# Swapped halves by small DMAs for the rotary embedding, instead of a rotation product

## The chip, the cores and the metric

The kernel runs on one core of a Trainium2 chip. The metric is the time of one execution in device microseconds. The text is about five engines of the core: TensorE (matrix products, PE in the profile), VectorE (DVE), ScalarE (ACT), GpSimd (POOL) and SyncE (SP), which here only issues DMAs. Each engine works through its own program in order; engines meet only at semaphores. A DMA's data is moved by 16 DMA engines once SyncE has issued it.

## The reference

Two blocks run on 512 tokens of width 1024. The second has two layers, each with four kinds of attention whose queries and keys partly get a rotary embedding:

```python
def apply_rope(z, cos, sin):
    ...
    z1, z2 = jnp.split(z, 2, axis=-1)
    return jnp.concatenate([z1 * c - z2 * s, z1 * s + z2 * c], axis=-1)
```

It is applied to heads of 64 columns (`cos_h`), to 32 columns of each latent-attention head (`cos_r`) and to index heads of 32 columns (`cos_i`). So every element is multiplied by a cosine, and the element half a head away, with a sign, by a sine; the two are added.

## The kernel before

All activations lie transposed in SBUF: features on the 128 partitions, 512 tokens in the free dimension. A head's two halves are therefore on different partitions, 32 or 16 rows apart.

**Weights** come as slabs of 8 tiles of 128 x 128 (512 KB) in the order of use. `load_slabs` (L521) lets SyncE fetch them into three raw buffers: slab n may be fetched when the buffer of slab n - 3 is free. For most slabs, ScalarE writes a rounded high half (`high_slabs`, L545, 128 x 1024) and GpSimd or VectorE the low half (`low_slabs`, L560); then the raw buffer is free (`w_lo_made`), and TensorE makes three products for each tile, high by high, high by low and low by high. A few slabs ("plain") are used unsplit in the two-pass format of 32 bits, and their buffer is free only when their last product is done (`sums_done`). In ScalarE's program the high half of the slab two ahead stands before the eviction of the job at hand, so the eviction waits if that slab has not landed.

**The feature stage** (`gemm_phase`, L611 and after, called by `Layer.features` with `banks=3` and `between=Features`) runs once in each of the two layers. Its jobs, in order: kvcmp, dki, iq0, iq1, cq0, cq1, ckv, kk, nq0, nq1, dq0, dq1, sq0, sq1 (8 tiles, 24 products each), then mq0 to mq3 (2 plain tiles), four uk jobs (1 plain tile each) and two token jobs (uv). A job sums into one of three PSUM banks, and ScalarE evicts it to its tile in `big` (L693, signals `taken`). Thirteen jobs have a rope: kvcmp, dki, iq0, iq1, kk, nq0, nq1, dq0, dq1 and mq0 to mq3. For these

- TensorE, after the products of the next job, multiplies the evicted tile by a 128 x 128 rotation matrix into bank 4 or 5 (`rotate`, L651, signals `rotated`);
- VectorE multiplies that bank by the sine table into a scratch tile (L714), the tile by the cosine table in place (L716), and adds the two (L718, signals `joined`).

Between jobs, `Features` puts work of its own: hidden products of the compression (L2556, plain slabs, after iq1, cq0, cq1 and ckv), index scores (L2690, evicted by L2699, added up by VectorE at L2714), sums of squares of two norms (L836, from squares at L865), halves of keys on GpSimd (L2754). It waits for `joined` counts where it needs roped tiles.

The order of each engine's program is what the loops write; there is no scheduler. At the end of the stage a barrier (L392) holds all engines until each is through, and attention begins (L1882 on TensorE), whose own jobs use the next slabs. The rope tables and rotation matrices (`rope`, 4608 columns) are loaded into `big` ahead of the stage (L753).

## Time and profile before

| | us |
|---|---|
| median of three runs | 3346.08 (3340.59 to 3346.92) |
| profiled execution, span from first to last instruction | 3349.0 |
| TensorE busy in the span | 3244.9 |
| VectorE busy | 1487.5 |
| ScalarE busy | 1272.6 |
| GpSimd busy | 384.3 |
| DMA, slabs of weights | 503 issues of 512 KB |

The profiled execution is one of its own; its span is 2.9 us above the median, and what lies outside the span is not shown. The busy time of an engine counts overlapping matmuls once. The granted clock of TensorE over the span is 0.989 of full speed. The stage that the change touches lasts about 120 us in each of the two layers, and ends at 1605 us and at 2729 us of the span.

### The profile page before, as it was taken

The numbers are of one execution on the slowest core, as the hardware profiler recorded it, in microseconds if no ns is written. First come the engines' busy times: TensorE is split into PE (matmuls) and PEld (weight loads), VectorE is DVE, ScalarE is ACT, GpSimd is POOL, SyncE is SP. The second block draws the span as 40 slices with busy tenths as digits, with TensorE's granted clock in tenths as the row PEclk, the third lists the DMA queues.
The fourth block names the chain that finished last, engine by engine and source line by source line (L and its number), as shares of the span: only waits on it lengthen the run. The fifth ranks groups of instructions, "written<-read, shape, count | busy, mean of one in ns | idle before, by whom it ended". The sixth has DMA issues, their size and how long they took to land. (4 is left out here: it accounts for less than half of the span.)

```text
span 3349.0 us, 37289 instructions
## 1 busy us (share of the span) xinstructions
PE 3244.9 (97%) x14860; PEld 2566.0 (77%) x14860; DVE 1487.5 (44%) x2324; ACT 1272.6 (38%) x2190; POOL 384.3 (11%) x277
## 2 busy tenths in 40 slices
PE   9999999999999999999979999999999998899998
PEld 7767678878888888877656888878887766578886
DVE  4154523244243333355875533343334478563333
ACT  3344643233232223235655423242222456542222
POOL 0411324410000000002510000000000243000000
PEclk9998999999999999999989999999999999999999
DMA  4211213323333333332001232323332310023332
GB/s 154 88 44 38 88 58 106 96 87 95 101 95 99 96 99 92 99 104 88 26 1 63 88 96 93 100 87 96 95 95 88 129 45 1 27 88 95 97 94 74
DMA packets 76061, 276.92 MB, mean 83 GB/s; under 512 B 8688, under 2 KB 8944, under 8 KB 75632
## 3 DMA queue, kind: packets, MB, share of 16 engines
q1 hardware_dynamic: 75888, 274.54, 26.5%
q8 instruction: 118, 1.93, 0.2%
q14 instruction: 55, 0.45, 0.0%
HBM read 272.41 MB, written 2.10 MB: 82 GB/s over the span
## 5 line engine op out<-in xcount | busy, mean ns | idle before, releaser
L545 ACT ACTIVATE w_hi<-raw_slabs 128x1024 fp32r<-128x1024 f32 x489 | 516.7, 1057 | 1236.5 <-PE ps L585 1128.8
L560 DVE TENSOR_TENSOR w_lo<-raw_slabs,w_hi 128x1024 fp32r<-128x1024 f32 x372 | 454.8, 1223 | 717.3 <-ACT w_hi L545 717.2
L585 PE MATMUL ps<-in_hi,w_hi 128*128 128x512 f32 x1840 | 719.5, 391 | 5.0 <-DVE in_lo L911 5.0
L585 PE MATMUL ps<-in_hi,w_lo 128*128 128x512 f32 x1840 | 716.3, 389 | 0.0
L585 PE MATMUL ps<-in_lo,w_hi 128*128 128x512 f32 x1840 | 716.2, 389 | 0.0
L585 PE MATMUL ps<-parts,w_hi 128*128 128x512 f32 x2240 | 693.9, 391 | 0.9 <-DVE scratch L1528 0.8
L560 POOL TENSOR_TENSOR w_lo<-raw_slabs,w_hi 128x1024 fp32r<-128x1024 f32 x117 | 287.7, 2461 | 2315.2 <-ACT w_hi L545 2298.1
L585 PEld LDWEIGHTS ps<-parts,w_hi 128*128 128x128 f32 x2240 | 420.5, 188 | 92.6 <-issue 4.3
L585 PE MATMUL ps<-parts,w_lo 128*128 128x512 f32 x1120 | 436.0, 389 | 0.0
L585 PEld LDWEIGHTS ps<-in_hi,w_hi 128*128 128x128 f32 x1840 | 345.5, 188 | 83.2 <-DVE in_lo L911 9.2
L585 PEld LDWEIGHTS ps<-in_lo,w_hi 128*128 128x128 f32 x1840 | 345.5, 188 | 72.0 <-issue 1.0
L585 PEld LDWEIGHTS ps<-in_hi,w_lo 128*128 128x128 f32 x1840 | 345.5, 188 | 71.6
L585 PEld LDWEIGHTS ps<-parts,w_lo 128*128 128x128 f32 x1120 | 210.3, 188 | 43.6
L667 PE MATMUL ps<-in_hi,w_hi 128*128 128x512 f32 x584 | 236.8, 405 | 1.6 <-POOL w_lo L560 1.4
L667 PE MATMUL ps<-in_hi,w_lo 128*128 128x512 f32 x584 | 227.7, 390 | 0.0
L667 PE MATMUL ps<-in_lo,w_hi 128*128 128x512 f32 x584 | 227.7, 390 | 0.0
L1314 DVE SCALAR_TENSOR_TENSOR big<-ps,scratch 128x512 f32<-128x512 f32 x88 | 60.6, 691 | 267.8 <-PE ps L585 248.6
L667 PEld LDWEIGHTS ps<-in_hi,w_hi 128*128 128x128 f32 x584 | 109.7, 188 | 32.0 <-issue 6.8
L667 PEld LDWEIGHTS ps<-in_lo,w_hi 128*128 128x128 f32 x584 | 109.7, 188 | 25.4 <-issue 3.8
L667 PEld LDWEIGHTS ps<-in_hi,w_lo 128*128 128x128 f32 x584 | 109.7, 188 | 23.3
L2059 ACT ACTIVATE scratch<-ps,stats 128x384 f32<-128x384 f32 (+4 forms) x176 | 85.3, 485 | 99.7 <-DVE stats L2032 73.2
L1890 PE MATMUL ps<-const_cols,scratch 128*128 128x128 f32 (+1 forms) x472 | 94.1, 295 | 20.6 <-ACT scratch L1938 17.3
(303 smaller groups left out, 3579.4 us busy)
## 6 DMA issues: line engine op xcount, KB each, us to landing
raw_slabs<-weights SPq DMA_DIRECT2D x503, 512.0 KB, 3.6
big<-rope SPq DMA_DIRECT2D x2, 2304.0 KB, 8.8
x_resid<-xT SPq DMA_DIRECT2D x8, 256.0 KB, 5.0
outT<-x_resid SPq DMA_DIRECT2D x8, 256.0 KB, 2.0
const_cols<-consts SPq DMA_DIRECT2D x1, 836.0 KB, 9.6
scratch<-brow SPq DMA_DIRECT2D x1, 768.0 KB, 9.4
vector_cols<-vec SPq DMA_DIRECT2D x2, 45.5 KB, 9.9
vector_cols<-vec SPq DMA_DIRECT2D x1, 68.5 KB, 3.1
```

The costliest lines, as they stand in the source:

```text
L545: self.nc.scalar.activation(self.w_hi[:, m % SPLIT, :], self.raw[:, n % RAW, :], ACT.Copy)\
L560: (self.nc.gpsimd if i is None else self.nc.vector).tensor_tensor(self.w_lo[:, m % SPLIT, :], self.raw[:, n % RAW, :], self.w_hi[:, m % SP ...
L585: mm = k.nc.tensor.matmul(out, lhsT, rhs, start=(c == 0 and m == 0), stop=(last and m == 2))
L667: mm = nc.tensor.matmul(k.ps[:, bank + j % banks, cols], lhsT, rhs, start=(start and m == 0), stop=(stop and m == len(part) - 1))
L1314: nc.vector.scalar_tensor_tensor(made(f), k.ps[:, 2 * (f % 3) + 1, :], 0.5, k.scr[:, f % 2, :], ALU.mult, ALU.mult).then_inc(hidden, 1)
L1890: mm = k.nc.tensor.transpose(k.ps[0:w, bank, a:a + P], p[:, a:a + w], k.c("ident"))
L2059: nc.scalar.activation(probs(i)[:, 0:u.width], k.ps[:, bank(i), 0:u.width], ACT.Exp, bias=col(0, i), scale=u.scale, accum_out=col(1, i)).t ...
```

## The change

The rotation matrices and the rotation products go. In their place SyncE copies the halves of the evicted tile, crosswise, into the scratch tile: for each head (span) of n rows, two DMAs of n/2 rows by 512 elements (`ROPE_SPANS`; 4 for a tile of two 64-row heads, 2 for kvcmp, of which 64 rows are roped, 8 for iq0 and iq1, 6 for dki, 2 for each mq job). The sine table carries the minus sign of the first half. VectorE waits for the copies (`swapped`, two semaphores in turn), multiplies the scratch tile by the sine table in place, and goes on as before; for the mq jobs it now works on the 32 rows 64 to 96. SyncE's program in this stage becomes: for each rope job, fetch the slabs up to three ahead of that job's (two for a plain one), wait for the eviction, from the third rope on wait for the sum of the rope two before, issue the copies; after the last, fetch the rest. The table has 4096 columns. Semaphores of the first stage get new names (`x_here` to `tile_here`), which is cut from the diff below.

```diff
@@ -236,8 +236,9 @@
 for _n in ("h2", "i4", "mq", "kx"):
     ROPE.add("cos_" + _n, T)
     ROPE.add("sin_" + _n, T)
-for _n in ("h2", "i4", "mq", "kx"):
-    ROPE.add("rot_" + _n, P)
+
+ROPE_SPANS = {"h2": ((0, 64), (64, 64)), "i4": tuple((32 * i, 32) for i in range(4)), "mq": ((64, 32),),
+              "kx": ((0, 64), (64, 32), (96, 32))}
 
 VEC1 = Columns()
 for _n, _w in (("norm1_g", 8), ("norm2_g", 8), ("b_mq", 4), ("b_mk", 4), ("b_mo", 4), ("b_fq", 4), ("b_fk", 4),
...
@@ -284,12 +276,10 @@
             ang = (np.arange(T, dtype=np.float32)[None, :] * inv.astype(np.float32)[:, None]).astype(np.float32)
             for half in range(2):
                 cos[a + half * n // 2:a + (half + 1) * n // 2] = np.cos(ang.astype(np.float64))
-                sin[a + half * n // 2:a + (half + 1) * n // 2] = np.sin(ang.astype(np.float64))
+                sin[a + half * n // 2:a + (half + 1) * n // 2] = (2 * half - 1) * np.sin(ang.astype(np.float64))
         return cos, sin
 
-    for kind, spans in (("h2", [(0, 64), (64, 64)]), ("i4", [(32 * i, 32) for i in range(4)]),
-                        ("mq", [(64, 32)]), ("kx", [(0, 64), (64, 32), (96, 32)])):
-        put("rot_" + kind, rotation(spans))
+    for kind, spans in ROPE_SPANS.items():
         cos, sin = tables(spans)
         put("cos_" + kind, cos)
         put("sin_" + kind, sin)
@@ -518,10 +508,10 @@
             self.last_sum[at // SLAB + slab] = self.sums
         return [self.sums - jobs + 1 + b for b in range(jobs)]
 
-    def load_slabs(self, sp):
+    def load_slabs(self, sp, upto=NSLABS):
 
         last = max(self.last_sum) if self.last_sum else -1
-        while self.loaded < min(NSLABS, last + 1 + RAW):
+        while self.loaded < min(NSLABS, last + 1 + RAW, upto + 1):
             n = self.loaded
             if n >= RAW and n - RAW in SPLIT_AT:
                 sp.wait_ge(self.lo_made, SPLIT_AT[n - RAW] + 1)
@@ -629,28 +619,34 @@
         ends += k.use([tiles_of(job)], by_slab=False)
         if between:
             between.use(j)
-    taken, rotated, joined, part = [k.flag(n) for n in ("taken", "rotated", "joined", "rope_part")]
+    taken, joined, part = [k.flag(n) for n in ("taken", "joined", "rope_part")]
+    swapped = [k.flag(f"tile_here{n}") for n in range(2)]
     ropes = [j for j, job in enumerate(jobs) if job.get("rope")]
+    moves, landed = [], [0, 0]
+    for r, j in enumerate(ropes):
+        moves.append([(to, to + half, n // 2) for a, n in ROPE_SPANS[jobs[j]["rope"]] if a < jobs[j]["rope_rows"].stop
+                      for to, half in ((a, n // 2), (a + n // 2, -(n // 2)))])
+        landed[r % 2] += 16 * len(moves[r])
+        jobs[j]["swaps"] = landed[r % 2]
     banks = banks or (4 if ropes or norm else 8)
 
     with k.block() as block:
         @block.sync
         def _(sp):
+            for r, j in enumerate(ropes):
+                slab = max(tiles_of(jobs[j])) // SLAB
+                k.load_slabs(sp, slab + (RAW if slab in SPLIT_AT else RAW - 1))
+                sp.wait_ge(taken, k.at(taken, j + 1))
+                if r >= 2:
+                    sp.wait_ge(joined, k.at(joined, r - 1))
+                for to, src, n in moves[r]:
+                    sp.dma_start(k.scr[to:to + n, 10 + r % 2, :], jobs[j]["out"][src:src + n]).then_inc(swapped[r % 2], 16)
             k.load_slabs(sp)
 
         @block.tensor
         def _(pe):
             if norm:
                 norm.tensor(pe)
-
-            def rotate(r):
-                job = jobs[ropes[r]]
-                pe.wait_ge(taken, k.at(taken, ropes[r] + 1))
-                if r >= 2:
-                    pe.wait_ge(k.flag("rope_part"), k.at(k.flag("rope_part"), 2 * r - 3))
-                nc.tensor.matmul(k.ps[:, 4 + r % 2, :], k.rope("rot_" + job["rope"]), job["out"],
-                                 start=True, stop=True).then_inc(rotated, 1)
-
             if between:
                 between.tensor(pe, -1)
             for j, job in enumerate(jobs):
@@ -667,12 +663,8 @@
                         mm = nc.tensor.matmul(k.ps[:, bank + j % banks, cols], lhsT, rhs, start=(start and m == 0),
                                               stop=(stop and m == len(part) - 1))
                 mm.then_inc(k.sums_done, 1)
-                if j - 1 in ropes:
-                    rotate(ropes.index(j - 1))
                 if between:
                     between.tensor(pe, j)
-            if len(jobs) - 1 in ropes:
-                rotate(len(ropes) - 1)
 
         @block.scalar
         def _(act):
@@ -708,10 +700,10 @@
                 for j in range(len(jobs) + 1):
                     if j - 1 in ropes:
                         r, job = ropes.index(j - 1), jobs[j - 1]
-                        rows = slice(0, job.get("rope_rows", P))
+                        rows = job["rope_rows"]
                         turned, to = k.scr[rows, 10 + r % 2, :], job["out"][rows]
-                        dve.wait_ge(rotated, k.at(rotated, r + 1))
-                        nc.vector.tensor_tensor(turned, k.ps[rows, 4 + r % 2, :], k.rope("sin_" + job["rope"])[rows],
+                        dve.wait_ge(swapped[r % 2], k.at(swapped[r % 2], job["swaps"]))
+                        nc.vector.tensor_tensor(turned, turned, k.rope("sin_" + job["rope"])[rows],
                                                 ALU.mult).then_inc(part, 1)
                         nc.vector.tensor_tensor(to, to, k.rope("cos_" + job["rope"])[rows], ALU.mult).then_inc(part, 1)
                         dve.wait_ge(part, k.at(part, 2 * r + 2))
@@ -730,7 +722,7 @@
         norm.passed()
     if between:
         between.passed()
-    k.passed(taken=len(jobs), rotated=len(ropes), joined=len(ropes), rope_part=2 * len(ropes))
+    k.passed(taken=len(jobs), joined=len(ropes), rope_part=2 * len(ropes), tile_here0=landed[0], tile_here1=landed[1])
 
 
 def token_phase(k, x, jobs, norm, loads=(), bias_here=None, first=0, taken="taken"):
...
@@ -3246,11 +3239,11 @@
         for key, i in at.items():
             scale = 64 ** -0.5 if key in ("nq0", "nq1", "dq0", "dq1", "sq0", "sq1") else 1.0
             jobs.append(feature_job(k, x, w[key], tile(i), rope=rope.get(key), scale=scale,
-                                    rope_rows=64 if key == "kvcmp" else P))
+                                    rope_rows=slice(0, 64 if key == "kvcmp" else P)))
         names = list(at)
         for h in range(HEADS):
             jobs.append(feature_job(k, lambda c: tile(6 + c), w["uq"][h], tile(25 + h), depth=2, split=False, rope="mq",
-                                    scale=96 ** -0.5))
+                                    rope_rows=slice(64, 96), scale=96 ** -0.5))
         for h in range(HEADS):
             jobs.append(feature_job(k, lambda c: tile(8), w["uk"][h], tile(29 + h)[0:64], depth=1, split=False,
                                     view=lambda at: at[0:64]))
```

**SyncE, feature stage of the first layer, iq1 and what follows.** `raw_slabs` are weights, `scratch<-big` the copies. Before, from the stage's start (L637) to the barrier (L392):

```order
L637 UNCONDITIONAL_BRANCH
L530 DMA raw_slabs<-weights 128x1024 [waits w_lo_made] x4
L530 DMA raw_slabs<-weights 128x1024 [waits sums_done]
L530 DMA raw_slabs<-weights 128x1024 [waits w_lo_made]
L530 DMA raw_slabs<-weights 128x1024 [waits sums_done]
L530 DMA raw_slabs<-weights 128x1024 [waits w_lo_made]
```

After, from dki's copies on:

```order
L643 DMA scratch<-big 16x512 x4
L520 DMA raw_slabs<-weights 128x1024 [waits w_lo_made]
L643 DMA scratch<-big 16x512 [waits joined,taken]
L643 DMA scratch<-big 16x512 x7
L520 DMA raw_slabs<-weights 128x1024 [waits w_lo_made]
L643 DMA scratch<-big 16x512 [waits joined,taken]
L643 DMA scratch<-big 16x512 x7
L520 DMA raw_slabs<-weights 128x1024 [waits sums_done]
L520 DMA raw_slabs<-weights 128x1024 [waits w_lo_made]
```

The fetch that waits for `sums_done` (slab 7, whose buffer the first hidden products free) now stands behind the eight copies of iq1 and their wait for its eviction.

**SyncE, end of the same stage.** Before:

```order
L530 DMA raw_slabs<-weights 128x1024 [waits sums_done]
L530 DMA raw_slabs<-weights 128x1024 [waits w_lo_made] x7
L530 DMA raw_slabs<-weights 128x1024 [waits sums_done] x2
L392 UNCONDITIONAL_BRANCH
L2007 UNCONDITIONAL_BRANCH [waits barrier_Pool_Activation_PE_DVE_SP_release]
```

After:

```order
L520 DMA raw_slabs<-weights 128x1024 [waits w_lo_made] x2
L643 DMA scratch<-big 16x512 [waits joined,taken]
L643 DMA scratch<-big 16x512
L643 DMA scratch<-big 16x512 [waits joined,taken]
L643 DMA scratch<-big 16x512
L643 DMA scratch<-big 16x512 [waits joined,taken]
L643 DMA scratch<-big 16x512
L643 DMA scratch<-big 16x512 [waits joined,taken]
L643 DMA scratch<-big 16x512
L520 DMA raw_slabs<-weights 128x1024 [waits sums_done] x2
L382 UNCONDITIONAL_BRANCH
```

The last two fetches, slabs 21 and 22, now stand behind the copies of the four mq jobs.

**TensorE, end of the same stage** (L667, in the change L663, `big,raw_slabs` are the products of the mq and uk jobs, L651 the rotations). Before:

```order
L2690 MATMUL ps<-parts 128x512 x3
L667 MATMUL ps<-big,raw_slabs 128x512 x2
L651 MATMUL ps<-big 128x512
L667 MATMUL ps<-big,raw_slabs 128x512 x2
L651 MATMUL ps<-big 128x512
L667 MATMUL ps<-big,raw_slabs 128x512 x2
L651 MATMUL ps<-big 128x512
L667 MATMUL ps<-big,raw_slabs 128x512
L651 MATMUL ps<-big 128x512
L667 MATMUL ps<-big,raw_slabs 128x512 x3
L667 MATMUL ps<-raw_slabs,big 128x128 x8
```

After:

```order
L2682 MATMUL ps<-parts 128x512 x3
L663 MATMUL ps<-big,raw_slabs 128x512 x10
L663 MATMUL ps<-raw_slabs,big 128x128 x8
L2556 MATMUL ps<-big,raw_slabs 128x31
L2558 MATMUL ps<-raw_slabs,big 31x64
```

The four rotations between the products of the mq and uk jobs are gone; nothing else changes its place on TensorE.

## Rows read from the trace of the kernel before

**Rows 1.** The page's head and busy time: engine, busy us (share), instructions.

```profile
span 3349.0 us, 37289 instructions
PE 3244.9 (97%) x14860; PEld 2566.0 (77%) x14860; DVE 1487.5 (44%) x2324; ACT 1272.6 (38%) x2190; POOL 384.3 (11%) x277
```

**Rows 2.** Line 651, rotations: count, duration min/median/max ns, first and last start.

```profile
L651 PE MATMUL ps<-big x52: 589/591/667, 1495.6 to 2722.9; 128*128 128x512 f32 x52
```

**Rows 3.** Timeline of TensorE, behind cq0: start us, us, engine, line, operation, count.

```profile
1516.40 1.02 PE L651 MATMUL ps<-big 128*128 128x512 f32 x2
1517.26 1.87 PE L2556 MATMUL ps<-big,raw_slabs 128*128 128x31 f32 x16
```

**Rows 4.** Timeline, iq1's eviction to cq1's first product; brackets: idle before, releaser.

```profile
1508.49 0.60 ACT L693 ACTIVATE big<-ps 128x512 f32<-128x512 f32 x1 [4.80 <-PE ps L667]
...
1514.76 1.06 ACT L545 ACTIVATE w_hi<-raw_slabs 128x1024 fp32r<-128x1024 f32 x1 [3.73 <-DMA raw_slabs<-weights]
1515.90 2.37 POOL L560 TENSOR_TENSOR w_lo<-raw_slabs,w_hi 128x1024 fp32r<-128x1024 f32 x1 [9.35 <-ACT w_hi L545]
...
1518.96 0.48 PE L667 MATMUL ps<-in_hi,w_hi 128*128 128x512 f32 x1
...
1511.04 0.80 SPq L530 DMA_DIRECT2D raw_slabs<-weights  x2
```

**Rows 5.** SyncE's issues: xT in the timeline; outT by line, with time to landing.

```profile
2.11 3.28 SPq L3017 DMA_DIRECT2D x_resid<-xT  x7
...
L1249 SPq DMA_DIRECT2D outT<-x_resid x8: 332/332/348, 3338.3 to 3346.6; - x8
...
DMA to landing us min/median/max: 2.0/2.0/2.0
```

**Rows 6.** Timeline behind nq0: squares on ScalarE, their sums on TensorE.

```profile
1546.32 1.67 ACT L865 ACTIVATE scratch<-big 128x512 f32<-128x512 f32 x3
...
1547.39 1.88 PE L836 MATMUL ps<-scratch,const_cols 128*128 128x512 f32 x4
```

**Rows 7.** Timeline of TensorE behind sq0 (with dq1's rotation) and behind sq1 (without).

```profile
1576.26 1.02 PE L651 MATMUL ps<-big 128*128 128x512 f32 x2
...
1578.37 0.39 PE L667 MATMUL ps<-in_hi,w_hi 128*128 128x512 f32 x1
...
1583.81 0.84 PE L2690 MATMUL ps<-parts 128*128 128x512 f32 x3
...
1585.48 1.88 PE L667 MATMUL ps<-big,raw_slabs 128*128 128x512 f32 x4
```

**Rows 8.** Timeline, end of the stage; last row: slab 21's copy in the second layer.

```profile
1592.37 4.62 POOL L2754 TENSOR_TENSOR parts<-big,parts 64x512 fp32r<-64x512 f32 x3
...
1594.12 0.68 DVE L714 TENSOR_TENSOR scratch<-ps,big 128x512 f32<-128x512 f32 x1
1594.72 1.15 DVE L716 TENSOR_TENSOR big<-big 128x512 f32<-128x512 f32 x1
...
1594.95 0.33 SPq L530 DMA_DIRECT2D raw_slabs<-weights  x1
...
1595.90 1.64 DVE L718 TENSOR_TENSOR big<-big,scratch 128x512 f32<-128x512 f32 x1
...
1598.63 1.06 ACT L545 ACTIVATE w_hi<-raw_slabs 128x1024 fp32r<-128x1024 f32 x1 [3.08 <-DMA raw_slabs<-weights]
1598.78 0.69 DVE L718 TENSOR_TENSOR big<-big,scratch 128x512 f32<-128x512 f32 x1
...
1605.46 0.38 PE L1882 MATMUL ps<-big 128*128 128x32 f32 x2 [1.16 <-PEq L392]
...
2722.59 1.06 ACT L545 ACTIVATE w_hi<-raw_slabs 128x1024 fp32r<-128x1024 f32 x1 [2.91 <-DMA raw_slabs<-weights]
```

**Rows 9.** Stretches of 1 us: busy by engine, granted clock (PEclk), DMA share, GB/s.

```profile
1609.00:1610.00 1.00, 1.00 (x8) 1.00 (x6) 0.39 (x2) 1.00 (x3) 0.43 (x2) 0.50 0.51 188
1610.00:1611.00 1.00, 1.00 (x4) 0.67 (x4) 0.97 (x5) 1.00 (x5) 0.07 (x1) 0.50 0.72 295
1611.00:1612.00 1.00, 1.00 (x4) 0.41 (x2) 0.92 (x3) 0.68 (x5) 0.91 (x1) 0.59 0.02 8
```

More of the change, by code:

```diff
@@ L269, in constants @@
     put("negroot", -np.eye(4) * np.sqrt(128.0))
-    def rotation(spans):
-        r = np.zeros((P, P))
-        for a, n in spans:
-            for i in range(n // 2):
-                r[a + n // 2 + i, a + i] = -1
-                r[a + i, a + n // 2 + i] = 1
-        return r
     def tables(spans):
@@ L3010, in copy_in_phase @@
     norm.lands = False
-    tile_here = [k.flag(f"x_here{c}") for c in range(KD)]
+    tile_here = [k.flag(f"tile_here{c}") for c in range(KD)]
     first_here, here = k.flag("norm_here"), k.flag("inputs_here")
@@ L3058, in _ @@
                 .then_inc(s["sq_summed"], 1)
+    k.passed(**{f"tile_here{c}": 16 for c in range(KD)})
     return here, 16 * len(later)
@@ L3215, in layer_start @@
     token_phase(k, lambda c: (k.in_hi[:, c, :], k.in_lo[:, c, :]), [(w["v"], lambda tb: big[:, tb, :], None)], ln1,
-                loads=[(big[:, 33:42, :].rearrange("p a b -> p (a b)"), k.rope_dram)], first=QB, taken="laid")
+                loads=[(big[:, 33:41, :].rearrange("p a b -> p (a b)"), k.rope_dram)], first=QB, taken="laid")
 class Layer:
```

## The prediction

> **What bounds the kernel now.** I read the page's table of engines first: TensorE is busy for 3244.9 of 3349.0 us [rows 1], so what leaves it shortens the kernel and what makes it wait lengthens it. Then I read only the stage that the diff touches, once per layer: twenty weight slabs, from about 1484 to 1605 us in the first layer. I number its slabs 0 to 22, where 20 to 22 belong to the attention stage. Fourteen feature jobs use split slabs (kvcmp 0, dki 1, iq0 2, iq1 3, cq0 5, cq1 7, ckv 9, kk 11, nq0 12, nq1 13, dq0 14, dq1 15, sq0 16, sq1 17), the hidden products of the compression use slabs 4, 6, 8, 10 unsplit, and four query jobs (mq0 to mq3) with the uk and uv jobs use 18 and 19. In this stage I followed two things: which row starts late because of a weight slab, and what the last instruction before the stage's barrier waited for.
>
> **The rotations leave TensorE.** There are 26, each of two passes, 52 rows of 591 ns [rows 2]. Passes overlap, so the price is the distance to what follows: 1516.40 to 1517.26, 0.86 us [rows 3]. 26 x 0.86 = 22.4 us is the most that leaving can give. Whether it is given has to be asked place by place, because slabs and evictions set a pace of their own. I do this for one layer and double it; the second layer's trace shows the same waits (its copy of slab 21 waited 2.91 us, the first layer's 3.08 [rows 8]).
>
> **SyncE gets a second job.** It loaded slabs as soon as buffers came free. Now each rope job puts in its program a wait for the eviction (taken), from the third rope on a wait for the sum two ropes back (joined), and 2 to 8 swap DMAs: 52 per layer. Everything queued behind is late by that, the next slab above all. The trace has no such small DMA. Its price of issue lies between the row of outT, 0.33 us busy each, and the seven back-to-back xT loads, 3.28 us for 7, or 0.47 each [rows 5]; the swaps' source is SBUF like outT's and their rows are as long as xT's, so I take 0.42. Landing: 2.0 us, outT's, is an upper value for a smaller copy within SBUF [rows 5]. It hardly enters the sum: for long jobs VectorE before waited until the next job's products were through, over 5 us, and a swap arrives after 0.42 x 4 + 2.0 = 3.7 us.
>
> **First place, iq1 and slab 7.** Slabs 7 and 8 are asked for at 1511.04, when slab 4 comes free. ScalarE's copy of slab 7 idled 3.73 us for it and began at 1514.76, GpSimd's low half ran 2.37 us from 1515.90 to 1518.27, and TensorE started cq1 at 1518.96 [rows 4]. So from the request to a usable slab it is 7.2 us, with 0.7 us to spare. Four rotations stand before cq1 (3.44 us). In the changed kernel slab 7 is behind iq1's eight swaps. Its eviction starts at 1508.49 and takes 0.60 [rows 4]; two rotations less before it, it ends at 1507.4. Add 0.1 for the wait and 8 x 0.42 = 3.4: the request goes out at 1510.9, where it was before. cq1 can then start at about 1510.9 + 7.2 + 0.1 = 1518.2. TensorE, ready at 1518.96 - 3.44 = 1515.5, waits 2.7 us. Of 3.44 us **0.75 is kept**; by 0.33 to 0.47 a swap, 1.4 to 0.3.
>
> **Middle, kk to dq1.** Here a slab is requested over two jobs ahead, and 4 swaps (1.7 us) are covered by a job of 1583.81 - 1578.37 = 5.44 us [rows 7]. Five rotations: kk's hid a wait. After it come sums of squares that need ScalarE's squares, three in 1.67 us from 1546.32, so the second is ready at 1547.43; the sums began at 1547.39 [rows 6]. The first may start 0.4 us sooner, no more: 0.43. Those of nq0 and nq1 give 0.86 each. Those of dq0 and dq1 stand ahead of four score products, the fourth of which waits for ScalarE: with a rotation it takes 1578.37 - 1576.26 = 2.11 us from the end of the job to the next, without one, behind sq1, 1585.48 - 1583.81 = 1.67 [rows 7]. They give 0.44 each. **3.0 us kept**. So at sq1's end TensorE is 3.8 us ahead, not 7.7.
>
> **Last place, the four mq jobs and slab 21.** Times are those of before, as if nothing had moved until there. Slab 21 was asked for at 1594.95, when mq3's products freed slab 18. ScalarE, in program order, must copy slab 21 before it evicts the uk jobs: it idled 3.08 us and copied at 1598.63; TensorE got over the barrier and began attention at 1605.46 [rows 8]. In the changed kernel this request stands behind mq3's swaps, and these wait for mq1's sum on VectorE. VectorE came to mq0 at 1594.12 [rows 8], so no swap makes it late, and finished mq0 at 1595.90 + 1.64 = 1597.5 and mq1 at 1598.78 + 0.69 = 1599.5 [rows 8]. Two of the three instructions of mq0 were slowed by GpSimd, which worked from 1592.37 to 1596.99: 1.15 and 1.64 us for 0.68 [rows 8]. The one that read PSUM wasn't slowed; it now reads two SBUF tiles as they do, so I add 0.75 and get 1600.25. Then 0.1 for the wait and 2 x 0.42: slab 21 is asked for at 1601.2, 6.25 us later than before. From there ScalarE needs 3.7 us for landing, as before, and the rest followed in 1605.46 - 1598.63 = 6.8 us. TensorE, without rotations, has three uk jobs done by then, which takes some 0.5 off. The barrier comes **5.75 us later** (4.7 with neither slowing nor dear issues, 6.5 with 0.47 and an extra half microsecond). That includes everything that the four rotations there give: they are hidden behind ScalarE's wait.
>
> The Trainium skill (SBUF — State Buffer, Who interferes with whom) states that a VectorE instruction with two SBUF inputs and a GpSimd instruction that reads SBUF block each other for a whole instruction, and one with a PSUM input does not. By that rule the swap's multiplication is slowed, which speaks against the change; without it the forecast would be 1.5 us lower over both layers.
>
> **The clock.** TensorE stands still behind this ScalarE wait. Slab 21's request marked the end of mq3's products, 1594.95; without two rotations that is 1593.2, and three uk jobs of two passes, 0.86 each, are through by 1595.8. The fourth needs a bank that ScalarE frees at about 1601.2 + 3.7 + 1.06 + 0.6 = 1606.5. That is over ten microseconds. Before the change a stretch with little work around the barrier was followed by a granted clock of 0.50, the 1.2 GHz level, at 1609 to 1611, and 0.59 in the next microsecond [rows 9]: it lost 0.5 + 0.5 + 0.4 = 1.4 us there. I expect another such loss, 1.5 us with the start of the stretch, on uk3 and the uv jobs; between 0 and 3.
>
> **Costed at nothing.** The cosine and sum instructions stay. The table without the rotations is shorter, and is loaded behind earlier jobs. The mq ropes work on 32 rows in place of 128 with the same 512 elements a row; I take the same time, and if they were shorter it would shift slab 21 by a few tenths at most.
>
> **Sum.** Per layer -0.75 - 3.0 + 5.75 + 1.5 = +3.5, less 0.17 for a wait of ckv that goes: +3.3 us. Twice: +6.6 us. The span would go from 3349.0 to 3355.6. The span is 2.9 us over the median of the runs, 3346.08, so the median should be 3352.7, say 3353.
>
> **Rivals.** (A) *Cheap swaps*: SyncE issues one in about 0.1 us and the clock holds. Then slab 7 goes when slab 4 is free and 3.0 us is kept there; the end costs 4.7. -3.0 - 3.0 + 4.7 = -1.3 a layer, 3343 to 3344. The same place, dearer or cheaper: half-way prices give 3345 to 3351. For it: the busy time is 0.33 already with 128 rows, and these have 16 or 32. Against: no issue in the trace is shorter. (B) *SyncE's order does not bind*: slab 21 reaches ScalarE in time, because mq1's sum comes sooner than I think. It would decide if the request were out by about 1595, 6 us before my reckoning. Then only VectorE's chain ends the stage, swaps of mq2 and mq3 in it, at about 1604.6, 0.6 us before the old end of the stage. 2 x (3.8 + 0.6) = 8.8 us faster, 3337; with all rotations given in full and none of the waits, 22.4 us faster, 3324. Against: the order of SyncE's program, and that ScalarE idled there already. (C) *Worse*: swaps at 0.6 us or slabs that land later behind them, a clock loss of 3 us and another one in the 2.7 us stall before cq1. +7 us a layer, 3360.
>
> **How the numbers follow.** My sum 0.5 (its bounds 3348 to 3358), A with its half-way prices 0.25, B 0.1, C 0.15. Range for 8 in 10: 3340 to 3362. A measurement of this kernel tells about 0.2% (6.7 us) from no change; my sum lies on that line. Slower by more: C and half of my sum, 0.42 with a little for what I overlooked. Within: the other half and nearly all of A, 0.44. Faster: B and the edge of A, 0.14.
>
> **What would show it.** In the trace of after: SyncE's request for slab 21 some 6 us after mq3's products; ScalarE's copy of it with an idle time near 9 us in place of 3.08; TensorE idle for about ten microseconds just before the last uk job, and a granted clock of 0.5 behind that; a wait of 2 to 3 us before cq1's first product, on GpSimd's low half; score products behind dq0 and dq1 waiting for ScalarE as sq1's do. It is wrong if the issue of a swap is well under 0.33 us, if the stage's end comes before the old one, or if VectorE waits for swaps for long in the middle.

## The result, and the profile after

| | us |
|---|---|
| the changed kernel, median of 4 runs | 3361.68 (3360.77 to 3368.57) |
| the kernel before, 4 runs | 3343.34 (3338.18 to 3346.92) |
| ratio | 1.0063, 95% interval 1.0048 to 1.0078 |
| span of the profiled execution, before and after | 3349.0, 3359.8 |

The change makes the kernel slower by 0.5 to 0.8%: 18.3 us between the medians, where 6.6 were forecast. The profiled spans differ by 10.8 us only, for a reason outside the change: in the profiled execution of before, TensorE ran for some 17 us in the first block at a granted clock of 0.50, in that of the changed kernel it did not. Stretches of both (us; busy time by engine; granted clock; DMA share; GB/s), before first:

```profile
255.00:260.00 5.00, 5.00 (x15) 2.85 (x15) 1.22 (x5) 1.47 (x6) 0.00 (x0) 0.50 0.00 0
```

```profile
250.00:275.00 25.00, 25.00 (x126) 15.26 (x125) 13.83 (x51) 11.84 (x42) 0.00 (x0) 1.00 0.00 1
```

Runs of one kernel fall into two groups some 8 us apart, and the profiled executions fit this stretch being cold or not. So I compare mainly **the length of the feature stage** in the trace, from its first eviction to attention's first product. Times inside a stage are counted from that eviction, and a stop is time in which TensorE stands idle. Before, it is 1605.46 - 1490.35 = 115.11 us in the first layer and 114.89 in the second; after, 123.64 and 124.96. The two differences, 8.53 and 10.07, make 18.6 us, which is what the medians show.

The evictions divide them (first layer / second layer, us, after minus before):

| part of the stage | first | second | forecast |
|---|---|---|---|
| to cq1's first product | +1.00 | +1.57 | -0.75 |
| cq1's products, to its eviction | +2.70 | +2.19 | 0 |
| from there to mq0's eviction | -2.82 | -2.59 | -3.0, with ckv's wait -3.17 |
| from there to attention | +7.65 | +8.90 | +7.25, clock included |

The page's head and busy time of the changed kernel (as in [rows 1]), and the copies by line (count; duration min/median/max in ns; first and last start) with their time to landing:

```profile
span 3359.8 us, 37289 instructions
...
PE 3225.0 (96%) x14808; PEld 2560.1 (76%) x14808; DVE 1493.1 (44%) x2324; ACT 1271.8 (38%) x2190; POOL 384.5 (11%) x277
```

```profile
L643 SPq DMA_DIRECT2D scratch<-big x104: 507/589/1667, 1481.6 to 2726.1; - x104
...
DMA to landing us min/median/max: 1.9/2.0/3.4
```

TensorE's busy time fell by 19.9 us, though in slow stretches its rows are longer, and the span grew. The landing is as taken in the median (2.0 us, up to 3.4), the issue isn't. The first place shows it; this is the timeline of the changed kernel that answers to [rows 4] (start us, us, engine, line, operation, count, idle before with its releaser):

```profile
1498.14 4.93 SPq L643 DMA_DIRECT2D scratch<-big  x8
1503.12 7.69 SPq L520 DMA_DIRECT2D raw_slabs<-weights  x4
```

```profile
1506.98 1.06 ACT L535 ACTIVATE w_hi<-raw_slabs 128x1024 fp32r<-128x1024 f32 x1 [7.12 <-DMA raw_slabs<-weights]
```

```profile
1508.11 2.34 POOL L550 TENSOR_TENSOR w_lo<-raw_slabs,w_hi 128x1024 fp32r<-128x1024 f32 x1 [9.75 <-ACT w_hi L535]
```

```profile
1504.40 1.86 PE L2548 MATMUL ps<-big,raw_slabs 128*128 128x31 f32 x16
1510.60 0.77 PE L663 MATMUL ps<-in_hi,w_hi 128*128 128x512 f32 x1 [4.34 <-POOL w_lo L550]
1511.16 0.63 PE L663 MATMUL ps<-in_lo,w_hi 128*128 128x512 f32 x1
1511.59 0.63 PE L663 MATMUL ps<-in_hi,w_lo 128*128 128x512 f32 x1
```

iq1's eight copies take 4.93 us, 0.62 each, so slab 7 is asked for 22.13 us after the stage's first eviction, where it was 20.69 before. TensorE is through with the hidden products and stops for 4.34 us. In the second layer the eight copies begin 0.5 us later, behind slab 6's fetch, slab 7 is asked for at 22.62 us, and the stop is 4.91 us. Then comes what the sum had at nothing: cq1's products start 0.43 us apart (1511.16 to 1511.59). Further on in the same job they are 0.23 apart. The granted clock of these stretches says why:

```profile
1508.00:1510.00 2.00, 0.00 (x0) 0.00 (x0) 1.04 (x1) 1.00 (x4) 1.89 (x1) 0.87 0.52 213
1510.00:1512.00 2.00, 1.40 (x3) 1.17 (x4) 0.87 (x1) 0.98 (x1) 1.39 (x2) 0.50 0.33 53
1512.00:1514.00 2.00, 2.00 (x6) 1.61 (x5) 0.00 (x0) 0.00 (x0) 1.43 (x1) 0.50 0.56 213
1514.00:1516.00 2.00, 2.00 (x6) 1.54 (x6) 0.00 (x0) 0.00 (x0) 0.00 (x0) 0.50 0.01 4
1516.00:1518.00 2.00, 2.00 (x10) 1.60 (x9) 0.00 (x0) 0.00 (x0) 0.00 (x0) 0.92 0.00 0
```

Full speed up to 1508 us, 0.87 in the next two microseconds, in which TensorE stands, then 0.50, the 1.2 GHz level, from 1510 to 1516, and 0.92 in the last row. The end of the stage in the changed kernel, to be read beside [rows 8]:

```profile
1583.90 4.61 POOL L2746 TENSOR_TENSOR parts<-big,parts 64x512 fp32r<-64x512 f32 x3
...
1585.74 1.64 DVE L706 TENSOR_TENSOR scratch<-scratch,big 32x512 f32<-32x512 f32 x1
...
1591.01 0.68 DVE L710 TENSOR_TENSOR big<-big,scratch 32x512 f32<-32x512 f32 x1
1592.41 0.68 DVE L706 TENSOR_TENSOR scratch<-scratch,big 32x512 f32<-32x512 f32 x1 [0.72 <-DMA scratch<-big]
1592.95 10.89 SPq L520 DMA_DIRECT2D raw_slabs<-weights  x2
...
1596.88 1.06 ACT L535 ACTIVATE w_hi<-raw_slabs 128x1024 fp32r<-128x1024 f32 x1 [11.51 <-DMA raw_slabs<-weights]
...
1598.47 2.07 PE L663 MATMUL ps<-big,raw_slabs 128*128 128x512 f32 x2 [11.16 <-ACT big L685]
...
1604.63 0.38 PE L1874 MATMUL ps<-big 128*128 128x32 f32 x2 [1.16 <-PEq L382]
```

mq1's sum is through at 1591.7 (L710, 1591.01 + 0.68), two more pairs of copies follow, and slab 21 is asked for at 1592.95. TensorE stands for 11.16 us, and runs uk3 and the first uv products at half speed:

```profile
1598.00:1601.00 3.00, 2.53 (x6) 1.50 (x7) 0.00 (x0) 1.80 (x4) 0.00 (x0) 0.50 0.00 0
1601.00:1604.00 3.00, 2.48 (x18) 2.15 (x17) 0.00 (x0) 1.75 (x5) 0.00 (x0) 0.89 0.00 0
```

### The profile page after: what moved, and what is told of

Read it like the earlier page. It is cut to its first block and busy times, and to the rows that moved or that the text cites. A ratio compares the mean times of both kernels' runs of the same rounds, so it can differ in the third digit from the quotient of the medians.

```text
span 3359.8 us, 37289 instructions
## 1 busy us (share of the span) xinstructions
PE 3225.0 (96%) x14808; PEld 2560.1 (76%) x14808; DVE 1493.1 (44%) x2324; ACT 1271.8 (38%) x2190; POOL 384.5 (11%) x277
## 5 line engine op out<-in xcount | busy, mean ns | idle before, releaser
L663 PE MATMUL ps<-in_hi,w_hi 128*128 128x512 f32 x584 | 237.5, 407 | 11.6 <-POOL w_lo L550 11.6
L663 PE MATMUL ps<-in_lo,w_hi 128*128 128x512 f32 x584 | 229.4, 393 | 0.0
L663 PE MATMUL ps<-in_hi,w_lo 128*128 128x512 f32 x584 | 229.2, 392 | 0.0
L663 PEld LDWEIGHTS ps<-in_hi,w_hi 128*128 128x128 f32 x584 | 110.9, 190 | 41.8 <-issue 15.0
L663 PEld LDWEIGHTS ps<-in_lo,w_hi 128*128 128x128 f32 x584 | 111.0, 190 | 25.0 <-issue 2.9
L663 PEld LDWEIGHTS ps<-in_hi,w_lo 128*128 128x128 f32 x584 | 110.8, 190 | 23.9
## 6 DMA issues: line engine op xcount, KB each, us to landing
scratch<-brow SPq DMA_DIRECT2D x1, 768.0 KB, 10.1
```

The source lines that it names most:

```text
L663: mm = nc.tensor.matmul(k.ps[:, bank + j % banks, cols], lhsT, rhs, start=(start and m == 0), stop=(stop and m == len(part) - 1))
```

## Experiments

My theory after the result: the rotations' time is given back because SyncE's program delays two slab fetches, slab 7 by the price of eight issues and slab 21 by waits and copies, and because each of the two stops so made is followed by products at half the clock. The rivals: the copies cost by their data or their landing; a third place loses; the clock has nothing to do with it. Stage lengths are given as first layer / second layer.

### Slab 7 asked for ahead of iq1's copies

```diff
-                k.load_slabs(sp, slab + (RAW if slab in SPLIT_AT else RAW - 1))
+                k.load_slabs(sp, slab + (RAW if slab in SPLIT_AT else RAW - 1) + (r == 3))
```

> The changed kernel with one thing moved: SyncE asks for slab 7 before it waits for iq1's eviction and issues iq1's eight copies. Theory 1 (order: the slab is late because its request stands behind the copies, and the stop in front of cq1 takes the clock down with it): the request goes out about 4 us sooner, TensorE waits under 1 us before cq1 in place of 4.3 and 4.9, and the granted clock of 0.5 behind it is gone; 6 to 7 us a layer, 12 to 14 us less than the changed kernel, about 3348. Theory 2 (the copies themselves: their traffic or their landing slows slabs and VectorE): the copies are all still there, so under 3 us less. Theory 3 (order, but the clock falls whatever the wait): only the wait goes, 3.9 us a layer, 8 us less.

Measured: 3349.19 us, ratio to before 1.0014 (1.0004 to 1.0023), stage 120.00 / 118.79. The stop before cq1 is 1.1 and 1.2 us. In the first layer the clock fell all the same, to 0.63 and 0.52 at 1516 to 1520, and cq1's eviction comes 9.79 us behind cq0's; in the second it is 8.40. So 12.5 us between the medians (0.49% by the two ratios to before), and 3.6 + 6.2 = 9.8 us of stage, hang on the place of one fetch. That the stop didn't go altogether is taken up with the run of one copy below.

### Slab 21 asked for ahead of the last two jobs' copies

```diff
-                k.load_slabs(sp, slab + (RAW if slab in SPLIT_AT else RAW - 1))
+                k.load_slabs(sp, slab + (RAW if slab in SPLIT_AT or r >= len(ropes) - 2 else RAW - 1))
```

> The changed kernel with one thing moved: SyncE asks for slab 21 before the copies of mq2 and mq3. Theory 1: the request goes out at the end of mq3's products, 8 us sooner; ScalarE no longer idles 11.5 us, and VectorE's chain through the mq ropes ends the stage, about 7 us sooner a layer, plus 1 to 2 us for the clock: 14 to 17 us less than the changed kernel, about 3346. Theory 2 (copies themselves): under 3 us less. Theory 4 (VectorE's late mq sums, not ScalarE's wait for the slab, set the end of the stage already): no change within 2 us.

Measured: 3344.46 us, ratio 1.0007 (0.9996 to 1.0019), stage 114.38 / 116.21. TensorE's wait for ScalarE falls from 11.2 to 2.4 and 3.5 us, the one before cq1 stays at 4.3 and 5.1. The second place is worth 9.3 + 8.8 us of stage, the clock's part in it included: cq1's products took 7.17 and 7.82 us here, 8.45 and 7.95 in the changed kernel.

### Both fetches first

Both edits of the same line together.

> Both requests moved ahead, all copies kept. Theory 1: the gains add up, 26 to 30 us less than the changed kernel, 3331 to 3335, and so 8 to 13 us faster than the kernel before: per layer 3.0 us kept of the first four rotations, 3.0 of the next five, and nearly nothing at the end, where VectorE's chain of copies takes the place of the rotations. Theory 2: still slower than the kernel before.

Measured: 3333.99 us, **ratio 0.9975 (0.9963 to 0.9987)**, stage 109.84 / 109.56. This beats both kernels. The gains add up: 3.6 + 9.3 of stage make 12.9 in the first layer and 6.2 + 8.8 make 15.0 in the second; 13.8 and 15.4 came. Nothing of the copies themselves was changed, neither their number nor their bytes, so the rival on data and landing falls for all but what this run still has above the next one. No third place loses either: from cq1's eviction to mq0's it takes 60.7 us here and in the changed kernel.

### No rotation at all

```diff
-                k.load_slabs(sp, slab + (RAW if slab in SPLIT_AT else RAW - 1))
-                sp.wait_ge(taken, k.at(taken, j + 1))
-                if r >= 2:
-                    sp.wait_ge(joined, k.at(joined, r - 1))
-                for to, src, n in moves[r]:
-                    sp.dma_start(k.scr[to:to + n, 10 + r % 2, :], jobs[j]["out"][src:src + n]).then_inc(swapped[r % 2], 16)
             k.load_slabs(sp)
...
-                        dve.wait_ge(swapped[r % 2], k.at(swapped[r % 2], job["swaps"]))
+                        dve.wait_ge(taken, k.at(taken, j + 1))
```

> The changed kernel without any copy and without SyncE's waits for them; VectorE multiplies whatever the scratch tile holds, once the next job is evicted. So the rotation is left out altogether. It measures what taking the rotations off TensorE is worth when nothing takes their place. Theory 1: 16 to 18 us faster than the kernel before, 3326, not the 22.4 us of 26 rotations, because slab 7's arrival, the squares and the score products take their part. If all of 22.4 us came, my place-by-place count of what is kept would be wrong.

Measured: 3330.08 us, ratio 0.996 (0.9946 to 0.9975), stage 108.93 / 107.80. With no copy and no rotation the stage is 6.2 and 7.1 us shorter than before, and not 11.2 (22.4 by two). The run with both fetches first is 0.9 and 1.8 us short of it. In the first layer VectorE's last sum (it ended at 1590.4 us, attention began at 1590.76) held the barrier, at which TensorE stood 2.47 us, 1.15 in the second layer; so leaving alone might give about a microsecond more there, an estimate that no run shows.

### The first stop filled

A stop can be filled with work that changes nothing:

```diff
+                if ropes and j == 5:
+                    k.keep_busy(pe, 18, bank=4)
                 if j >= banks:
                     pe.wait_ge(taken, k.at(taken, j - banks + 1))
```

> The changed kernel with one addition: before cq1's wait for slab 7's low half TensorE makes 18 products of 512 columns with an identity matrix into PSUM bank 4, which nothing reads; the output is the same. They last about as long as the stop of 4.3 to 4.9 us there. Theory (the stop costs twice: once as a wait, and once more because the granted clock is 0.50 while cq1's first products run): the slabs come as late as in the changed kernel, the eviction of cq1 follows that of cq0 in 8.3 us in place of 11.1, the stage of the first layer lasts about 121 us in place of 123.6, and the time is 5 to 6 us under the changed kernel's, 3355 to 3357. Rival (the slow cq1 comes from late weights and not from the clock): no gain, 3361 to 3362, or a microsecond more where the added products outlast the stop.

Measured: 3352.88 us, ratio 1.0040 (1.0025 to 1.0055), stage 121.04 / 121.90. Timeline of TensorE, then the stretch behind:

```profile
1506.80 4.35 PE L396 MATMUL ps<-masks 128*128 128x512 f32 x18
1511.37 0.47 PE L665 MATMUL ps<-in_hi,w_hi 128*128 128x512 f32 x1 [0.23 <-POOL w_lo L550]
1511.68 0.40 PE L665 MATMUL ps<-in_lo,w_hi 128*128 128x512 f32 x1
1511.91 0.39 PE L665 MATMUL ps<-in_hi,w_lo 128*128 128x512 f32 x1
```

```profile
1512.00:1514.00 2.00, 2.00 (x11) 1.65 (x10) 0.00 (x0) 0.71 (x1) 1.21 (x1) 1.00 0.87 213
```

In the first layer cq1 starts 29.68 us after the stage's first eviction, as in the changed kernel (29.61), and yet its products take 5.73 us in place of 8.45 (before: 5.75). Only the clock differs. In the second layer they take 5.73 in place of 7.95. This is the cleanest number for it: **the stops of 4.3 and 4.9 us cost 2.7 and 2.2 us more behind them.** The stage is 2.6 and 3.1 us shorter; in the second layer 0.4 of that comes from slab 7, asked for 0.46 us sooner there, and another 0.4 falls at the stage's end. The price isn't fixed: with slab 21 asked for first, stops of 4.34 and 5.13 us were followed by losses of 1.4 and 2.1. The median fell by 8.8 us, 3 us more than the two stages give; between the two stages this execution took 1006.9 us, the changed kernel's 1010.1, before 1009.2. That part I can't assign.

### Both stops filled

48 more such products before uk3.

> As the last one, and 48 such products before uk3, where TensorE waits 11 us for ScalarE's evictions. The output is the same. Theory: besides the 5 to 6 us of the first stop, the second cold stretch (6.8 us at a granted clock near 0.5 in the changed kernel, of which 3.4 us or so are there before the change too) goes as well, 1.7 to 3 us a layer: 3350 to 3353. The wait for slab 21 itself stays, so the time doesn't fall below that. Rival (only waits cost, not the clock): 3361 to 3362.

Measured: 3352.49 us (3348.86 to 3358.03), ratio 1.0043 (1.0026 to 1.0060), stage 119.36 / 119.52. The second stop's clock is worth 1.7 and 2.4 us of stage. The medians of this run and the last don't tell them apart; the stages do. From the uk0 eviction to attention it took 5.25 us in both layers, in the changed kernel 6.79 and 8.07. So in all the clock's part of the loss is 2.7 + 1.5 = 4.2 us of 8.5 in the first layer and 2.2 + 2.8 = 5.0 of 10.1 in the second. The kernel before loses none of this inside the stage: its granted clock falls behind attention's first product only [rows 9].

### SyncE's order alone

The kernel before, rotations kept, with the changed program of SyncE but no copies:

```diff
+            for r, j in enumerate(ropes):
+                slab = max(tiles_of(jobs[j])) // SLAB
+                k.load_slabs(sp, slab + (RAW if slab in SPLIT_AT else RAW - 1))
+                sp.wait_ge(taken, k.at(taken, j + 1))
+                if r >= 2:
+                    sp.wait_ge(joined, k.at(joined, r - 1))
             k.load_slabs(sp)
```

> The kernel before, rotations kept on TensorE, with the changed kernel's program on SyncE but for the copies: for each rope job it fetches the slabs up to that point, waits for the eviction and for the sum two ropes back, and copies nothing. Theory: at the first place this costs nothing (iq1's eviction is through at 1509.1, and slab 7's buffer comes free only at 1511.0); at the end slab 21 stands behind mq1's sum, 1599.5 in place of 1594.95, so the stage ends some 4 us later, 119 us in place of 115, with 0 to 1.5 us of clock on top: 3349 to 3353. Rival (it is the DMAs and not the waits that cost): within 1 us of the kernel before, 3341 to 3343. Other rival (a wait in SyncE's program costs everywhere): over 3355.

Measured: 3360.66 us (3352.91 to 3361.55), ratio 1.0057 (1.0042 to 1.0072), stage 121.83 / 121.54, so +6.7 and +6.7. Up to mq3 every eviction is where it was to 0.2 us, cq1's at 34.36 us in both. At the end of the stage, SyncE, ScalarE and TensorE in the timeline:

```profile
1596.26 11.91 SPq L533 DMA_DIRECT2D raw_slabs<-weights  x2
...
1599.95 1.06 ACT L548 ACTIVATE w_hi<-raw_slabs 128x1024 fp32r<-128x1024 f32 x1 [7.74 <-DMA raw_slabs<-weights]
...
1601.53 2.08 PE L681 MATMUL ps<-big,raw_slabs 128*128 128x512 f32 x2 [3.80 <-ACT big L707]
```

SyncE asks for slab 21 with the end of mq1's sum on VectorE (1595.40 + 0.69 = 1596.1). The uk0 eviction comes 9.30 us after mq3's in place of 4.64, and the rest of the stage takes 8.06 us in place of 5.87: 4.7 of waiting and 2.2 of clock. That is above the 4 us and up to 1.5 that I expected. The median is 21.5 us over the 3339.13 of before beside it, where the stages give 13.4. In the profiled execution the first stage began at 1487.14 us of the span, 5.5 us later than in the run with the first stop filled (1481.69), so part of the rest lies ahead of the stages; they are what I go by.

### The copies added to that

The same with 52 copies a layer from a constant into a spare tile, of the same rows and 56 columns. SyncE also waits, ahead of each job's copies, until those of the job before have landed, which the changed kernel doesn't do.

> As the last one, with the 52 copies a layer issued as well, of the same rows, but of 56 columns of a constant into a spare tile that nothing reads; rotations stay on TensorE and VectorE never waits for a copy. Theory: the copies' issues cost 0.6 us each also with short rows, so slab 7 is asked for 3 us later than before, 1514, and cq1 waits 2.4 us more, with a clock loss of up to 2.7 us behind it; slab 21 goes 1.2 us later than in the last run. Together 3 to 5 us a layer over the last run: 3356 to 3363. If issue goes by bytes, the short rows make it cheap, and the time stays within 2 us of the last run.

Measured: 3371.53 us, ratio 1.0093 (1.0078 to 1.0108), stage 127.07 / 126.63: 5.2 and 5.1 us over the last run, just past the 3 to 5 I expected. The median is 32.4 us over the 3339.13 of before, where the stages give 23.7; here the first stage began at 1489.49 us of the span. The copies by line, and TensorE's wait before cq1 in the timeline:

```profile
L658 SPq DMA_DIRECT2D spare_tiles<-masks x104: 507/589/817, 1490.1 to 2738.3; - x104
...
DMA to landing us min/median/max: 1.6/1.7/2.5
```

```profile
1520.96 0.47 PE L692 MATMUL ps<-in_hi,w_hi 128*128 128x512 f32 x1 [2.69 <-POOL w_lo L564]
```

A copy of 224 bytes a row costs SyncE as much as one of 2048: minimum and median of the issue are the same to the nanosecond, and only the landing is 0.3 us shorter. cq1's eviction is 4.5 us later than before: its first product starts 2.85 us later, behind a stop of 2.69 us (slab 7 was asked for 3.04 us later), and its products take 1.6 us longer, as here too the granted clock fell, to 0.56 and 0.59 at 1522 to 1526. At the end of the stage slab 21 is asked for 1.5 us later than in the last run, counted from mq0's eviction; 0.4 of this is the added wait for mq2's landing (1.74 us from 1601.63), which makes this run's second place dearer than copies alone would.

### One copy instead of eight for iq0 and iq1

```diff
+        if jobs[j]["rope"] == "i4":
+            moves[r] = [(0, 0, P)]
```

> The changed kernel, where for iq0 and iq1 one DMA copies all 128 rows straight (not crosswise) in place of eight DMAs of 16 rows; so these two tiles get a wrong rotation, and as many bytes are moved by an eighth of the issues. Theory (the number of issues sets the price, 0.62 us each): slab 7 is asked for 4.3 us sooner, the stop before cq1 goes to at most 1 us as it did when slab 7 was asked for first, and the slow products behind it go too: cq1's eviction 8.0 to 8.8 us behind cq0's, the stage 118 to 120 us, the time 8 to 12 us under the changed kernel's, 3350 to 3354. Rival (bytes or the landing set it): slab 7 is asked for within 1 us of where it was, the stop stays above 3 us, 3359 to 3362.

Measured: 3350.40 us (3342.80 to 3354.93), ratio 1.0016 (1.0003 to 1.0030), stage 117.20 / 116.46.

```profile
1498.11 0.50 SPq L645 DMA_DIRECT2D scratch<-big  x1
1499.19 0.84 SPq L520 DMA_DIRECT2D raw_slabs<-weights  x2
```

SyncE's timeline: 128 rows in one issue take 0.50 us, no more than 16 rows. Slab 7 goes out 4.1 us sooner, the stop falls to 0.4 us or less and the clock holds. The stage gains 6.4 and 8.5 us, 2.8 and 2.3 more than when slab 7 was merely asked for first. SyncE asked for it at the same time in both runs, 18.02 us into the stage (first layer). But it took longer to land there, where the eight copies stood right behind it. First that run, then this one (first layer, slab 7 alone):

```profile
1508.56 0.33 SPq L520 DMA_DIRECT2D raw_slabs<-weights  x1
DMA to landing us min/median/max: 4.7/4.7/4.7
```

```profile
1499.19 0.33 SPq L520 DMA_DIRECT2D raw_slabs<-weights  x1
DMA to landing us min/median/max: 3.4/3.4/3.4
```

The 1.3 us between them account for the stop of 1.1 us that stayed: the copies do have a cost by their data after all, on the slab just ahead of them. The rest of the gain is mostly clock: cq1's products took 1.4 us less in the first layer, and the stretch from uk0's eviction to attention 0.6 and 1.2 us less.

### Both fetches first, and the last stop filled

```diff
+                if ropes and j == 21:
+                    k.keep_busy(pe, 12, bank=4)
                 if j >= banks:
```

> Slabs 7 and 21 both asked for first, as in the third run, and 12 products of 512 columns into an unread bank before uk3, where TensorE stands 2.7 us for ScalarE and the granted clock falls to 0.65 and 0.50 behind it. The output is the same. Theory: the wait stays, the clock holds; the stage goes from 109.8 to about 108 us, the time 2 to 4 us under the third run's ratio of 0.9975 to the kernel before, 0.9963 to 0.9970. Rival (the clock falls all the same at the barrier): 0.9975, no gain.

Measured: 3335.13 us, ratio 0.9960 (0.9947 to 0.9972), stage 109.62 / 111.97. From the uk0 eviction to attention it took 7.27 us in the first layer; without the added products 7.31. The clock held, but the wait moved to the barrier, as the timeline of TensorE and VectorE shows:

```profile
1580.84 3.33 PE L396 MATMUL ps<-masks 128*128 128x512 f32 x12
...
1589.75 0.68 DVE L712 TENSOR_TENSOR big<-big,scratch 32x512 f32<-32x512 f32 x1
...
1590.76 0.38 PE L1876 MATMUL ps<-big 128*128 128x32 f32 x2 [3.18 <-PEq L382]
```

VectorE's last sum ends at 1590.4 and the barrier opens behind it. So with both fetches in time it is VectorE's chain for the mq jobs that ends the stage, and neither the slabs nor the clock: from mq0's eviction to attention it took 16.9 us in all four layers of this run and the one without the products. The intervals of this run and of the one without the products overlap: no gain is shown. (In its second layer a stop of 0.87 us before cq1 was followed by a granted clock of 0.50, and cq1 came 9.9 us after cq0, where 8.4 is usual; this lengthens that stage.)

```profile
2626.00:2628.00 2.00, 2.00 (x6) 1.58 (x5) 1.08 (x2) 0.00 (x0) 0.00 (x0) 0.50 0.94 383
```

## Why the prediction failed in size

The sign of the likeliest case was right and 3361.68 lies inside the range, at its edge. The forecast of 3353 was 9 us too low, and the change in time nearly three times the forecast one (18.3 us where 6.6 were forecast; the forecast started from a median of 3346.08, the result has 3343.34). All four parts of the stage came out dearer than the sum had them, so no error hid another. By the steps:

- **Rotations, middle: right.** -3.17 a layer was the sum with ckv's wait, -2.8 and -2.6 came. ckv's wait of 0.2 us was there in the first layer only; the rest of the shortfall is at kk's rotation, 0.20 for 0.43, and nq1's, 0.49 for 0.86. The score products behind dq0 and dq1 wait for ScalarE as foreseen. That the most which leaving can give is far under 22.4 us is shown by the run without rotation: 6.2 and 7.1 us a layer.
- **Last place: right.** Slab 21 was to be asked for 6.25 us later; it was 6.5 later, counted from mq0's eviction. (As a sign I had named a request some 6 us after mq3's products. It was about 8, since these come sooner without the rotations, as the text on the clock had reckoned.) To attention +7.25 was the sum, 5.75 of waiting and 1.5 of clock; +7.65 and +8.90 came, 6.1 of waiting in both layers and 1.5 and 2.8 of clock. The run with the order alone shows that 4.7 us of waiting are the wait for mq1's sum, which needs no copy. The slowed sine multiplication is there too: L706 of mq0 took 1.64 us beside GpSimd's L2746, where L714, reading PSUM, took 0.68 beside the same work [rows 8]. Here the trace agrees with the Trainium skill (SBUF — State Buffer, Who interferes with whom): by its rule a VectorE instruction with two SBUF inputs contends with a GpSimd instruction that reads SBUF, one with at most one SBUF input doesn't. The 0.75 us added for it stands against 0.96 for that instruction. The three of mq0 together took 4.02 us in place of 3.43, 0.6 more, as the sum of mq0 (L710) now fell behind GpSimd's work and took 0.68 where it took 1.64 before.
- **First place: the step that failed, by its price.** The price of a swap's issue, "so I take 0.42", is 0.59 busy and 0.62 apart, outside the bounds of 0.33 to 0.47 that I took from outT's stores and xT's loads. Eight times 0.2 us is 1.6; with it -0.75 becomes +0.85, and +1.00 and +1.57 came, the second with copies that began 0.5 us later. The bounds were the fault: both rows were of one kind, DMAs between DRAM and SBUF, and I let them bound another kind. Whether it is the kind that makes the issue dearer no run shows.
- **First place: the clock, costed at nothing.** The sum had a stop of 2.7 us before cq1 and no loss behind it. The stop was 4.3 and 4.9 us, and the loss 2.7 and 2.2. At the end of the stage I had costed the same effect, and rival C had it here too; the sum left it out. The copies-added run shows that a stop of 2.7 us, as my own sum had it, can meet it as well: in both layers a stop of 2.69 was followed by a lower clock and 1.6 us of loss. So this was no matter of the issue price alone.

Added up: the first place is off by 4.45 + 4.51 us, the end by 0.4 + 1.65, the middle by 0.35 + 0.6; that is 11.9 of the 12.0 us between 6.6 and 18.6. Rival C, with issues of 0.6 us and a second clock loss, described what happened and gave 3360; it had a chance of 0.15. Rival B's condition, slab 21 in time, is made true by the run with slab 21 first; there the first place still cost 2.4 and 3.9 us against before, where B had 0.75 kept, and the ratio was 1.0007. With both fetches first, which goes beyond B as slab 7 comes sooner too, the stages are 10.6 us shorter than before where B had 8.8, and VectorE's chain ends the stage as B said.

## What to carry to other kernels

A DMA put into a queue that also fetches weights is paid for by the fetch behind it: price it by its count, not its bytes, and put due fetches ahead of it. Such copies right behind a fetch still hold up its landing, here by 1.3 us of 3.4. One changed line of SyncE's program turned +0.63% into -0.25%. When a sum leaves a stop of a few microseconds on TensorE, write a possible fall of the clock behind it into the sum, at each such place. And when a row of another kind bounds an unknown price, reach beyond it.

## What the runs showed of the hardware

- The issue of a copy within SBUF from SyncE takes 0.51 to 0.59 us, back to back 0.62 apart, alike for 224 and 2048 bytes a row; one of 128 rows takes 0.50. A slab of 512 KB takes 0.33, and 0.58 when it comes right behind such copies (1497.46 in the changed kernel):

```profile
1495.57 1.85 SPq L643 DMA_DIRECT2D scratch<-big  x3
1497.46 0.58 SPq L520 DMA_DIRECT2D raw_slabs<-weights  x1
```

- Slab 7 with the eight copies right behind it landed 4.5 to 5.3 us after its issue (six layers of the three runs that ask for it first), 3.4 and 3.6 us in the run of one copy, where the copy stands ahead of it and another slab right behind.
- Stops of TensorE of 4.3 us, of 2.7 us and, in one layer each, even of 1.1 and 0.87 us, right behind the hidden products (of 31 columns), were followed by a granted clock of 0.5 to 0.6 for 3 to 6 us. Other stops of 1.2 us in the same place (the second layer with slab 7 first, the first with both fetches first) weren't, so a stop's length alone doesn't decide it. What it cost in cq1's products was 1.4 to 2.7 us.
